# Strassen's scheme in half of the k pairs of two down projection column chunks

## The reference, cut to what matters

```
h = rmsnorm(x, ln_mlp_g[layer])
a = square(relu(h @ w_up[layer]))      # 256 x 8192
x = x + a @ w_down[layer]              # 256 x 2048
```

## Time and profile before

| | |
|---|---|
| median of 3 runs | 2108.58 us (2107.95 to 2109.29) |
| the profiled execution | 2109.32 us, span 2107.6 us |
| PE busy | 2094.4 us, 99% of the span, 10506 matmuls |
| VectorE, ScalarE, GpSimd busy | 1192.7, 996.4, 85.5 us |
| TensorE clock granted | 1.0 |
| DMA | 380.29 MB in the queue of the loads, 55.2% of the 16 engines' span |

### The profile page before, as it was taken

The page is one execution under the profiler, slowest core; times in us unless marked ns, Lnnn a source line. Parts: engine busy times, 40 slices in busy tenths (PEclk is TensorE's granted clock), DMA queues, the critical chain, the costliest instruction groups (busy, mean ns, idle before and its releaser), DMA issues.

```text
span 2107.6 us, 26856 instructions
## 1 busy us (share of the span) xinstructions
PE 2094.4 (99%) x10506; PEld 1775.1 (84%) x10506; DVE 1192.7 (57%) x1429; ACT 996.4 (47%) x1417; POOL 85.5 (4%) x133
## 2 busy tenths in 40 slices
PE   8999999999999999999999999999999999999999
PEld 7887888888888888888888898888888888888887
DVE  6545555565555546555555687556555555555654
ACT  5545564444344434434445676444434434443442
POOL 0000000000000000000000255000000000000000
PEclk9999999999999999999999999999999999999999
DMA  8545544555555555565655443555555556555553
GB/s 280 178 145 161 165 167 147 183 188 188 199 184 196 187 193 180 200 198 181 199 182 171 154 126 120 166 194 180 200 188 192 188 192 194 185 200 185 179 201 134
DMA packets 198477, 381.99 MB, mean 181 GB/s; under 512 B 10892, under 2 KB 17112, under 8 KB 198360
## 3 DMA queue, kind: packets, MB, share of 16 engines
q1 hardware_dynamic: 198312, 380.29, 55.2%
q10 hardware_dynamic: 48, 0.02, 0.0%
HBM read 378.19 MB, written 2.10 MB: 180 GB/s over the span
## 4 chain that ended last, share of the span: by engine, by line
PE 98%; DVE 1%; ACT 1%; DMA 0%; issue 0%; POOL 0%; SPq 0%; DVEq 0%; ACTq 0%; POOLq 0%
PE psum L1300 23%; PE psum L1231 19%; PE psum L1233 19%; PE psum L1232 19%; PE psum L1303 11%; PE psum L1364 1%; PE psum L1450 1%; PE psum L1318 0%; DVE halves L874 0%; PE psum L1427 0%; PE psum L1273 0%; PE psum L1451 0%; PE psum L1411 0%; PE psum L1412 0%; DMA x_tok<-in_x 0%; PE psum L1421 0%
## 5 line engine op out<-in xcount | busy, mean ns | idle before, releaser
L874 DVE TENSOR_TENSOR halves<-raw,halves 128x1024 fp32r<-128x1024 f32 (+1 forms) x724 | 883.1, 1225 | 741.7 <-ACT halves L590 740.4
L590 ACT CAST halves<-raw 128x1024 fp32r<-128x1024 f32 (+1 forms) x724 | 754.0, 1043 | 916.0 <-PE psum L1233 609.5
L1300 PE MATMUL psum<-h,halves 128*128 128x512 f32 x2048 | 639.8, 396 | 0.1
L1231 PE MATMUL psum<-halves,a 128*128 128x512 f32 x1340 | 525.8, 392 | 0.0
L1233 PE MATMUL psum<-halves,a 128*128 128x512 f32 x1340 | 522.2, 390 | 0.0
L1232 PE MATMUL psum<-halves,a 128*128 128x512 f32 x1340 | 521.9, 389 | 0.0
L1303 PEld LDWEIGHTS psum<-h,halves 128*128 128x128 f32 x2048 | 380.6, 188 | 86.9
L1303 PE MATMUL psum<-h,halves 128*128 128x256 f32 x2048 | 398.1, 278 | 0.0
L1300 PEld LDWEIGHTS psum<-h,halves 128*128 128x128 f32 x2048 | 314.1, 189 | 3.5 <-DVE halves L874 0.9
L1233 PEld LDWEIGHTS psum<-halves,a 128*128 128x128 f32 x1340 | 251.6, 188 | 52.6
L1231 PEld LDWEIGHTS psum<-halves,a 128*128 128x128 f32 x1340 | 251.7, 188 | 51.6 <-ACT nat L655 0.4
(11 more groups left out here) (193 smaller groups left out, 879.9 us busy)
## 6 DMA issues: line engine op xcount, KB each, us to landing
raw<-in_mlp_w_up SPq DMA_DIRECT2D x128, 1024.0 KB, 5.5
raw<-in_mlp_w_down SPq DMA_DIRECT2D x128, 1024.0 KB, 5.0
raw<-in_sf_w_in SPq DMA_DIRECT2D x45, 1024.0 KB, 5.1
raw<-in_sf_w_o SPq DMA_DIRECT2D x16, 1024.0 KB, 5.1
raw<-in_mla_w_o SPq DMA_DIRECT2D x16, 1024.0 KB, 5.0
raw<-in_mla_w_down SPq DMA_DIRECT2D x8, 1024.0 KB, 5.0
raw<-in_mla_w_ukv SPq DMA_DIRECT2D x8, 1024.0 KB, 5.2
raw<-in_mla_w_uq SPq DMA_DIRECT2D x8, 768.0 KB, 4.7
```

Of the source, the lines that this page charges most:

```text
L590: nc.scalar.copy(half_piece(n, 0), raw_piece(n)).then_inc(hi_done, 1)
L874: v.tensor_tensor(half_piece(n, 1), raw_piece(n), half_piece(n, 0).bitcast(F32), ALU.subtract)\
L1231: mm(bank, x_hi, hi[:, i], start=(k == 0), stop=False)
L1300: last = mm(bank, half_piece(n, 0)[:, cols], src[:, k].rearrange("p s t -> p (s t)"), start=(k == 0), stop=(k == KT - 1))
```

## The change

Take two neighbouring k tiles (y1, y2; each for token tiles 1 and 2) and the weights' rows of these tiles in two column chunks (b11, b12 above b21, b22). Their contribution to chunks 1 and 2 is a product of 2 x 2 blocks, which needs eight block products. Strassen's scheme (in Winograd's form) needs seven, of sums of blocks. The change uses it for four of the eight such "quads" (`FAST_QUADS` 0, 2, 4, 6) of the down chunks 1 and 2, in seven of the eight blocks of the two MLPs (`FAST`; not in the last block of layer 0). The other quads take eight plain products. Chunks 1 and 2 of a fast block thus run together, in all eight banks (X1 to X8), with quads in turn.

- **Pieces.** A fast quad has four: `raw` (b11 and b21; X1, X2), `t13` and `t24` (two weight sums each; X5, X7 and X6, X4) and `b22` (512 elements; X3): 6, 6, 6 and 3 matmuls. A plain quad has two of 12. A fast block has 72 pieces in place of 64, and these eight quads are pieces 40 to 63. The loads of the two chunks now come in pairs, and a slot is held through a fast and a plain quad.
- **Weight sums** (`weight_sums`, GpSimd). Per fast quad one subtraction of 1024 elements and two of 512, each behind the one before, once both loads are there. Two buffers in turn. ScalarE's split of `t13` waits for the first, that of `t24` for the third.
- **Token sums** (`token_sums`, VectorE). At the end of each up chunk four sums of 128 elements from `y_buf`, of which ScalarE makes the hi (512) and, two pieces later, VectorE the lo.
- **Combining** (`combine`, VectorE, with one copy of X1 by ScalarE). Twelve steps of 512 elements behind the splits of pieces 64 to 73 take the place of the four adds of chunks 1 and 2. The last down chunk, in the banks of X1 and X2, waits for step 3. The first up chunks of the next block wait for step 12 and for the last down chunk.

The core of the diff, in the order of the file: the plan, SyncE's wait, GpSimd's sums, ScalarE's two insertions (end of an up chunk; copy of X1), VectorE's sums and combining, PE's quad.

```diff
+FAST = (True, True, True, False), (True, True, True, True)
+PLAIN_PIECES, FAST_PIECES = 64, 72
+FAST_QUADS = 0, 2, 4, 6
+def pair_loads(layer, l):
+    first = block_load(layer, 0) + 20 + 2 * l
+    return (first, first + 1) if first % SLOTS != SLOTS - 1 else (first + 1, first)
+    for q in range(8):
+        one, two = (p + 32 * b0 for p in pair_loads(layer, q // 2))
+        if q in FAST_QUADS:
+            m = FAST_QUADS.index(q)
+            plan += [("raw", one, q % 2), ("t13", m, 0), ("t24", m, 0), ("b22", two, q % 2)]
+        else:
+            plan += [("raw", one, q % 2), ("raw", two, q % 2)]
...
-                    sp_.wait_ge(lo_done, 2 * load - 2 * SLOTS + 2 + 2 * extra)
+                    sp_.wait_ge(lo_done, LAST_OF[load - SLOTS] + 1 + extra)
...
+            def weight_sums(layer):
+                for b0 in range(sum(FAST[layer])):
+                    base, no = block_base(layer, b0), fast_no(layer, b0)
+                    for m, q in enumerate(FAST_QUADS):
+                        one, two = (p + 32 * b0 for p in pair_loads(layer, q // 2))
+                        done = 12 * no + 3 * m
+                        for load in (one, two):
+                            pool.wait_ge(raw_loaded[load % SLOTS], 16 * (load // SLOTS + 1))
+                        before = base + quad_at(FAST_QUADS[m - 2]) - (0 if m > 1 else FAST_PIECES)
+                        if m > 1 or b0:
+                            pool.wait_ge(lo_done, before + 3)
+                        at = q % 2 * 2 * N
+                        t = t_sum[m % 2]
+                        b11_b12 = raw[:, one % SLOTS:two % SLOTS + 1:two % SLOTS - one % SLOTS, at:at + N]
+                        b12_b22 = raw[:, two % SLOTS, at:at + 2 * N].rearrange("p (i n) -> p i n", i=2)
+                        b21 = raw[:, one % SLOTS, at + N:at + 2 * N]
+                        pool.tensor_tensor(t[:, 0:2], b12_b22, b11_b12, ALU.subtract).then_inc(t_step, 1)
+                        pool.wait_ge(t_step, done + 1)
+                        pool.tensor_tensor(t[:, 2], b12_b22[:, 1], t[:, 0], ALU.subtract).then_inc(t_step, 1)
+                        pool.wait_ge(t_step, done + 2)
+                        pool.tensor_tensor(t[:, 3], b21, t[:, 2], ALU.subtract).then_inc(t_step, 1)
...
+                    if fast:
+                        act.wait_ge(a_step, 16 * no + 4 * c + 4 + 16 * blk)
+                        nc.scalar.copy(sd[:, c, :, 0], a_sum).then_inc(sd_hi, 1)
...
+                    if fast and j == quad_at(6) + 1:
+                        act.wait_ge(pieces_used, base + quad_at(6) + 1 + FAST_PIECES * blk)
+                        nc.scalar.copy(c_sum[:, 0], X1).then_inc(x1_copied, 1)
...
+            def token_sums(no, c, blk):
+                done = 16 * no + 4 * c
+                y11, y21, y12, y22 = (y_buf[:, k, tt * P:(tt + 1) * P] for k in range(2) for tt in range(TT))
+                v.tensor_tensor(a_sum[:, 0], y21, y22, ALU.add).then_inc(a_step, 1)
+                v.tensor_tensor(a_sum[:, 2], y11, y21, ALU.subtract).then_inc(a_step, 1)
+                dve.wait_ge(a_step, done + 1 + 16 * blk)
+                v.tensor_tensor(a_sum[:, 1], a_sum[:, 0], y11, ALU.subtract).then_inc(a_step, 1)
+                dve.wait_ge(a_step, done + 3 + 16 * blk)
+                v.tensor_tensor(a_sum[:, 3], y12, a_sum[:, 1], ALU.subtract).then_inc(a_step, 1)
...
+                if step == 1:
+                    dve.wait_ge(x1_copied, no + 1 + blk)
+                    dve.wait_ge(pieces_used, used + FAST_PIECES * blk)
+                    v.tensor_tensor(p1_p6, X6, p1_p2, ALU.add).then_inc(combined, 1)
+                elif step == 2:
+                    after(1)
+                    v.tensor_tensor(p1_p6_p7, X7, p1_p6, ALU.add).then_inc(combined, 1)
+                elif step == 3:
+                    dve.wait_ge(pieces_used, used + FAST_PIECES * blk)
+                    v.tensor_tensor(p1_p2, X2, p1_p2, ALU.add).then_inc(combined, 1)
...
+                joined = {quad_at(6) + 2: (1,), quad_at(6) + 3: (2,), quad_at(7): (3,),
+                          quad_at(8): (4, 5), quad_at(8) + 1: (6,), quad_at(8) + 2: (7, 8), quad_at(8) + 3: (9,),
+                          quad_at(8) + 4: (10, 11), quad_at(8) + 5: (12,)}
...
+                    if base + j + AHEAD < P_END:
+                        split_lo(base + j + AHEAD, blk)
+                    if fast and j == 33:
+                        token_sums_lo(no, 3, blk)
+                    for step in joined.get(j, ()):
+                        combine(no, step, base + j + 1, blk)
...
+            def fast_quad(n, q, added, blk):
+                first, last = q == FAST_QUADS[0], q == FAST_QUADS[-1]
+                c = q // 2
+                s1, s2, s3, s4 = (tuple(sd[:, c, i, s] for s in range(2)) for i in range(4))
+                for i, parts in enumerate((((X1, tokens(2 * q, 0), 0), (X2, tokens(2 * q + 1, 0), 1)),
+                                           ((X5, s1, 0), (X7, s3, 1)),
+                                           ((X6, s2, 0), (X4, tokens(2 * q + 1, 1), 1)),
+                                           ((X3, s4, 0),))):
+                    pe.wait_ge(lo_done, n + i + 1 + FAST_PIECES * blk)
+                    if first and i == 3:
+                        pe.wait_ge(x_added, added + 4 * blk)
...
+                    if fast and c == 3:
+                        pe.wait_ge(combined, 10 * no + 3 + 10 * blk)
```

More of the change, by code:

```diff
@@ new lines, with block_base, block_load, fast_no @@
+L_MLP0 = P_MLP0 // 2
+L_MIX1 = L_MLP0 + 32 * NB
+L_MLP1 = L_MIX1 + (P_MLP1 - P_MIX1) // 2
+def block_base(layer, b0):
+    return (P_MLP0, P_MLP1)[layer] + sum(block_pieces(layer, b) for b in range(b0))
+def block_load(layer, b0):
+    return (L_MLP0, L_MLP1)[layer] + 32 * b0
+def fast_no(layer, b0):
+    return sum(FAST[0]) * layer + sum(FAST[layer][:b0])
+def pair_loads(layer, l):
+    first = block_load(layer, 0) + 20 + 2 * l
+    return (first, first + 1) if first % SLOTS != SLOTS - 1 else (first + 1, first)
@@ new lines, in block_plan @@
+def block_plan(layer, b0):
+    load = block_load(layer, b0)
+    plan = [("raw", load + j // 2, j % 2) for j in range(40)]
+    if not FAST[layer][b0]:
+        return plan + [("raw", load + j // 2, j % 2) for j in range(40, 64)]
+    for q in range(8):
[5 more added lines that the diff above has]
+            plan += [("raw", one, q % 2), ("raw", two, q % 2)]
+    return plan + [("raw", load + j // 2, j % 2) for j in range(56, 64)]
@@ new lines, in quad_at, with all_pieces, put @@
+def quad_at(q):
+    return 40 + sum(4 if p in FAST_QUADS else 2 for p in range(q))
+def all_pieces():
+    out, seen = {}, set()
+    def put(n, kind, load, half, count=0):
+        out[n] = (kind, load, half, kind in ("raw", "b22") and load not in seen, count)
+        if kind in ("raw", "b22"):
+            seen.add(load)
+    for n in range(P_MIX0, P_MLP0):
+        put(n, "raw", n // 2, n % 2)
+    for n in range(P_MIX1, P_MLP1):
+        put(n, "raw", L_MIX1 + (n - P_MIX1) // 2, n % 2)
+    for layer in range(2):
+        for b0 in range(NB):
+            for i, (kind, load, half) in enumerate(block_plan(layer, b0)):
+                count = 12 * fast_no(layer, b0) + 3 * load + (1 if kind == "t13" else 3) if kind[0] == "t" else 0
+                put(block_base(layer, b0) + i, kind, load, half, count)
+    return out
@@ L261, in build @@
         nat = sb("nat", [P, 2, TT, N])
+        with nc.sbuf_tensor("sd", [P, 4, 4, 2, P], F32R) as sd:
+            pass
         mix = sb("mix", [P, 8192])
@@ L404, in half_piece @@
                 return narrow_piece(n)[:, :, which]
-            return halves[:, n % SLOTS, which, 0:flat(kts, width)]
+            return halves[:, n % SLOTS, which, 0:N if PIECES[n][0] == "b22" else flat(kts, width)]
         gain_rows = [(ln_mlp_g.rearrange("l (k p) -> (l k) p", p=P), 0, 32),
@@ L464, in load_x, with mlp @@
+            def mlp(layer):
+                fast = sum(FAST[layer])
+                with sp_.Fori(0, fast) as b:
+                    mlp_block(layer, 0, b)
+                for b0 in range(fast, NB):
+                    mlp_block(layer, b0, 0)
             def load_x(s):
@@ L1178, in mlp_block @@
                                     ALU.subtract).then_inc(split_done, 1)
[L1179 to L1200, removed]
@@ new lines, in mlp_block @@
+                    if fast:
+                        token_sums(no, c, blk)
+                joined = {quad_at(6) + 2: (1,), quad_at(6) + 3: (2,), quad_at(7): (3,),
+                          quad_at(8): (4, 5), quad_at(8) + 1: (6,), quad_at(8) + 2: (7, 8), quad_at(8) + 3: (9,),
+                          quad_at(8) + 4: (10, 11), quad_at(8) + 5: (12,)}
+                ends = {39: 0, block_pieces(layer, b0) - 1: 3}
+                if not fast:
+                    joined, ends = {}, {39: 0, 47: 1, 55: 2, 63: 3}
@@ L1515, in mixer, with product, tokens, plain_quad @@
                         n += 1
```

(25 more changed lines are left out.)

191 lines of the change are left out of this document (144 added, 47 removed).

## The result

The changed kernel took 2123.0 us (median of 4 runs, 2121.87 to 2125.95), the kernel before 2108.9 in the same rounds: 1.0069 of its time, with a 95% interval of 1.0055 to 1.0082. It is 14.1 us slower where 7.9 was forecast.

What follows compares the result with a forecast made beforehand. The prediction took PE's matmuls to bound the MLP. Per block -2.72 + 0.65 + 3.2 = +1.1 us, seven blocks +7.9, so 2108.6 + 7.9 = 2116.5, said as 2116 us; range 2096 to 2128.

Steps and rivals of the forecast that it cites:

- The matmuls: Fast quads on PE: 12 matmuls less per block, 2.72 us, 19.0 us saved in seven blocks.
- Token sums: End of each up chunk, VectorE and ScalarE: hidden in a slack of 0.7 to 1.0 us, cost nothing.
- stores at the end: End of the kernel: stores of two output columns (512 KB) still land before the last one, cost nothing.
- steps of the last chunk: Other combining steps on VectorE in chunk 3's 2.72 us pieces, with three pieces of lead: cost nothing.
- Combining: Before the last down chunk: PE waits until VectorE has read X1, X2; 0.65 us per block, 4.5 us in all.
- The meeting: Fast quads: GpSimd's sums and VectorE's two-SBUF-input ops exclude each other; PE stands 3.2 us per block, between 0 and 4.8.
- the wait ahead of piece 44: First pair of quads: the split of 44 ends at 6.4, PE wants it at 4.76; PE stands 1.6 us.
- my walk: One block timed from the start of piece 40: PE stands 1.6 + 0.8 + 0.8 = 3.2 us per block.
- Layer 0: Every other pair fetches its two loads in the other order; the sums need both, so nothing changes.
- rival 3: Fast quads: sums come late, ScalarE waits for the second 512 sum; 6 us per block, 2136 us, chance 0.08.
- Rival 1: Fast quads: meetings cost less than the matmuls save; 2094 us without meeting cost, 2101 with part; chance 0.27.
- The budget: Per pair of quads: VectorE's 5.9 us plus GpSimd's 4.5 want 10.4 us of a shared resource in 10.2 us.

Runs made afterwards that it cites:

- the best version: Changed kernel with the weight sums moved from GpSimd to VectorE and combining step 3 ahead of the split of piece 66: 2091.8 us, ratio 0.9923 to the kernel before.
- the memsets: Changed kernel with GpSimd's sums replaced by memsets that read nothing: about as long, 2097.2 us; one short memset per sum, 2096.2 us.
- all three changes of order: Changed kernel, sums still on GpSimd: 1024 sum as two of 512, fourth pair's load order changed, combining step 3 ahead of the split: 2107.5 us, ratio 0.9996.

## Why the prediction was right, and where it was off

- **The matmuls.** 19.0 us is right: the version in which nothing stands for a split or for step 3 has its quads at 40.80 us, and is 16.4 us faster as a whole. Of the 2.6 between, the stand at the 8670th matmul is 1.6; the rest was not followed up.
- **Token sums, stores at the end, steps of the last chunk.** Taken at nothing. Right: the up chunks are unchanged but for the one stand, which is not at a fifth piece, and in the best version the last down chunk of nearly every fast block has its 21.8 us.
- **Combining.** Forecast 0.65 us per block from hand-over, hi, lo and the step itself. The trace has 0.56 to 0.79 and 0.1 more at the chunk's start, and the edit that moves the step takes off 5.6 us for seven blocks (2097.4 to 2091.8), 0.8 each: 1 us more in all than forecast.
- **The meeting.** The mechanism was right and is shown by the memsets. The size is the term that was too small: 3.2 us per block, where the quads' lengths give (318.5 - 1.8) / 7 - 40.8 - 0.6 = 3.8. That is 4.5 us more in seven blocks. The profiled execution lies 8.7 us above the forecast difference (16.6 against 7.9): these 4.5, some 0.7 of combining, the stand's 1.9 and the 1.8 at half clock, and the last two are in no term of the sum. The median lies 2.5 us lower, and no trace says which part is smaller there. By parts: the wait ahead of piece 44 was forecast 1.6 and was 0.95, since GpSimd's 1024 sum started 0.5 us later after piece 40's start than in my walk (709.29 less 707.44, 1.85 in place of 1.4) and the split of 43 slipped in ahead of it. The second and third were forecast 0.8 and were 1.05 to 1.6. So a walk of one case gives the class of cost, not its place: the three blockings shift when one of them moves.
- **Layer 0.** "The sums need both, so nothing changes" was wrong. The other order makes the fourth pair's loads land late, and the last wait there is rival 3, a late sum (3.42 us on ScalarE). It has the price of the meeting that it takes the place of, as the run that set the order right shows.
- **Rivals.** Rival 1's arithmetic, 2094 without any meeting, is 2096 to 2097 in the three runs that have none; combining (1 us more than forecast) and the stand (1.5 to 1.7) are the difference.
- **The budget.** 10.4 us wanted of 10.2 in a pair rightly said that PE would stand. On VectorE alone the same sums want about 8.9 of 10.2, and nothing stands. The budget does not say for how long PE stands: with all three changes of order GpSimd's same sums cost 2.5 us per block in place of 3.8 ((303.4 - 285.6) / 7, by the quads of that trace and of the best version). The size of 3.2 came of walking one case, and that it came within 0.6 is in part luck, since two of its three waits were too small and one too large.

What stays open: what PE waits for at the stand before the 8670th matmul, and why blocks of one program fall into two patterns (waits of 0.95, 1.1 and 1.1 us, or 0.95, 0.3, 1.3 and 1.5).

## What to carry to other kernels

Before work is given to an idle GpSimd, add its time to that of VectorE's instructions with two SBUF inputs in the same stretch, as if they were one engine, and compare the sum with the stretch. Here the cheaper engine for "free" work was the busy one, since VectorE does in 2.6 us what GpSimd, by the forecast's estimate, shuts it out for 4.5 to do. Here 10.4 us wanted in 10.2 brought waits, and 89% of a stretch brought none; how long the waits are hangs on the order, and has to be measured. An instruction that frees a PSUM bank belongs ahead of one that only fills a buffer four pieces ahead. And when fetches are put in order, look at when each slot comes free in every turn of the ring, not only in the one that waits.

## What the runs showed of the hardware

- **Clock.** After longer or repeated waits PE was granted half its clock (1.2 in place of 2.4 GHz) for a while. This is the stretch in the changed kernel, after waits of 1.2 and 1.4 us with three matmuls between them; the clock is the third last column.

```profile
1544.60:1548.70 4.10, 3.94 (x10) 3.15 (x11) 4.10 (x4) 0.04 (x1) 1.25 (x1) 0.58 0.68 205
```

  Matmuls there came every 0.43 us in place of 0.23. Another block of the same execution had the same two waits and kept its clock. With the first sum twice there were nine such stretches, up to 10 us long, and with the changed load order one of 7. A short wait can thus cost more than itself.
- **GpSimd's memset.** In the version with memsets 1024 elements took 957 ns, and VectorE's splits kept a mean of 1235 ns. A GpSimd instruction that only writes did not hold them up; the sums, which read SBUF too, did.
